# One sink exponential per banded step, one key group on another score bank, final scales two additions sooner

## The reference

```
q,k,v = rope(rmsnorm(x) @ w_in)            # banded heads a, differential heads b
# banded attention: m = max(max_k s, sink)
p     = exp(s - m);  denom = sum(p) + exp(sink - m)
oa    = (p / denom) @ v                    # 8 heads, 2 key/value heads, window of 3 chunks of 64
# differential attention: a = softmax(s1) - lam * softmax(s2);  ob = rmsnorm(a @ v)
h = x + concat[oa, ob] @ w_out
h = h + crossattn(rmsnorm(h), memory)      # 4 heads, 256 memory rows
h = h + square(relu(rmsnorm(h) @ w_up)) @ w_down
y = rmsnorm(h) * g_final
```

## Time and profile before

| what | value |
|---|---|
| median of the runs | 1824.55 us (1822.61 to 1825.99) |
| the profiled execution's own time | 1830.64 us |
| its span | 1828.8 us |
| PE busy | 1745.8 us (95%) |
| DVE busy | 879.7 us (48%) |
| ACT busy | 547.3 us (30%) |
| POOL busy | 179.6 us (10%) |

### The profile page before, as it was taken

One profiled execution on the slowest core, in us unless ns is written; L12 is line 12 of the kernel. 1 busy time (PEld: TensorE's weight loads), 2 busy tenths in 40 slices (PEclk: granted clock), 3 DMA queues, 4 the chain that ended last, 5 costly groups with the idle time before them and its releaser, 6 DMA issues.

```text
span 1828.8 us, 29483 instructions
## 1 busy us (share of the span) xinstructions
PE 1745.8 (95%) x11905; PEld 1612.9 (88%) x11905; DVE 879.7 (48%) x1707; ACT 547.3 (30%) x1216; POOL 179.6 (10%) x355
## 2 busy tenths in 40 slices
PE   6998989997898999989999999999999999999997
PEld 6997989886787999988799999999999999999996
DVE  5556656665466345124323644444444444444445
ACT  5123344576555123025402422111111222112212
POOL 2113322112122001100000000000000000000002
PEclk9999999999999999999999999999999999999999
DMA  6322322254575406256151101111011111110102
GB/s 214 108 67 60 87 85 87 76 164 163 178 235 205 138 24 247 94 187 226 53 197 47 47 27 43 46 46 46 24 45 46 46 46 46 46 46 25 56 1 104
DMA packets 107533, 170.40 MB, mean 93 GB/s; under 512 B 7545, under 2 KB 75769, under 8 KB 107417
## 3 DMA queue, kind: packets, MB, share of 16 engines
q1 hardware_dynamic: 79512, 126.78, 20.4%
q0 software_dynamic: 8160, 22.29, 3.6%
q10 hardware_dynamic: 19760, 19.92, 3.4%
HBM read 138.17 MB, written 31.72 MB: 93 GB/s over the span
## 4 chain that ended last, share of the span: by engine, by line
PE 87%; DVE 4%; ACT 3%; issue 2%; DMA 2%; POOL 1%; SPq 0%; ACTq 0%; DVEq 0%; POOLq 0%
PE banks L2023 27%; PE banks L1977 24%; PE banks L2412 21%; PE banks L2178 2%; PE banks L2121 2%; PE banks L2300 2%; PE banks L2248 1%; PE banks L1965 1%; PE banks L2208 1%; PE banks L2280 1%; PE banks L2269 1%; ACT probs L1285 1%; DMA w_raw<-in_cache_mem_k 1%; PE banks L2158 1%; DVE xt_lo L1478 1%
## 5 line engine op out<-in xcount | busy, mean ns | idle before, releaser
L1977 PE MATMUL banks<-w_hi,xt_hi 128*128 128x256 f32 x1224 | 354.7, 290 | 17.2 <-DVE xt_lo L1478 4.8
L1977 PE MATMUL banks<-w_lo,xt_hi 128*128 128x256 f32 x1224 | 344.7, 282 | 0.0
L1977 PE MATMUL banks<-w_hi,xt_lo 128*128 128x256 f32 x1224 | 344.5, 281 | 0.0
L2023 PE MATMUL banks<-xt_hi,w_hi 128*128 128x384 f32 x960 | 323.0, 336 | 0.0
L2023 PE MATMUL banks<-xt_hi,w_lo 128*128 128x384 f32 x960 | 322.7, 336 | 0.0
L2023 PE MATMUL banks<-xt_lo,w_hi 128*128 128x384 f32 x960 | 322.6, 336 | 0.0
L1977 PEld LDWEIGHTS banks<-w_hi,xt_hi 128*128 128x128 f32 x1224 | 232.6, 190 | 26.2 <-issue 8.9
L1090 ACT ACTIVATE w_hi<-w_raw 128x2048 fp32r<-128x2048 f32 (+1 forms) x85 | 120.2, 1430 | 418.8 <-PE banks L2412 225.8
L1901 DVE TENSOR_TENSOR h<-h,banks 128x512 f32<-128x512 f32 x288 | 191.9, 683 | 98.9 <-PE banks L2412 96.8
L1977 PEld LDWEIGHTS banks<-w_lo,xt_hi 128*128 128x128 f32 x1224 | 232.9, 190 | 0.0
L1977 PEld LDWEIGHTS banks<-w_hi,xt_lo 128*128 128x128 f32 x1224 | 232.7, 190 | 0.0
(11 more groups left out here) (220 smaller groups left out, 2215.4 us busy)
## 6 DMA issues: line engine op xcount, KB each, us to landing
w_raw<-in_w_up SPq DMA_DIRECT2D x16, 1024.0 KB, 5.4
w_raw<-in_w_down SPq DMA_DIRECT2D x16, 1024.0 KB, 4.9
w_raw<-in_w_xkv ACTq DMA_DIRECT2D x8, 1024.0 KB, 6.1
kc_diff<-in_cache_diff_k SPq DMA_DIRECT2D x16, 512.0 KB, 5.6
vc_diff<-in_cache_diff_v SPq DMA_DIRECT2D x8, 1024.0 KB, 5.4
w_raw<-in_cache_mem_k SPq DMA_DIRECT2D x16, 512.0 KB, 7.6
w_raw<-in_w_in ACTq DMA_DIRECT2D x7, 1024.0 KB, 5.3
scaled<-mix_d SPq DMA_DIRECT2D x9, 512.0 KB, 5.2
```

What stands on the lines that cost most here:

```text
L1977: last = mm(out, xt[:, k, tok:tok + P], w[:, k, :], start=(k == 0 and n == 0), stop=(k == KD - 1 and n == 2))
L2023: last = mm(out, w[:, k, :], xt[:, k, tok:tok + CH], start=(k == 0 and n == 0), stop=(k == KD - 1 and n == 2))
```

## The change

The four exponentials of the sinks in a banded step of the prompt become one over four columns. For that DVE adds the sinks to the negative maxima of all four heads (a new tile `sunk`, a new semaphore `s_sunk`), behind the second half's minimum. The streams' banded steps keep theirs. The fourth group of head 2 goes to bank 1, with the waits that this bank needs. The final scales of tiles 3 to 7 stand elsewhere among the last additions.

```diff
@@ banks of the key groups
+PREP[I_D2 - 1][1] = (PREP[I_D2 - 1][1][0], 1)
@@ build
         esink = sb("esink", [P, 4, 4])
+        sunk = sb("sunk", [P, 4, 4])
...
+        s_sunk = sem("s_sunk")
@@ prepared_on
-            on = [n for n, (m, _, b) in enumerate(PREP_LIST) if I_D2 <= m < i < I_X and b in score_banks(i, j)]
-            last = [[n for n in on if (PREP_LIST[n][1][0] == "mem") == low][-1:] for low in (False, True)]
+            on = [n for n, (m, _, b) in enumerate(PREP_LIST) if I_D2 - 1 <= m < i < I_X and b in score_banks(i, j)]
+            last = [[n for n in on if (PREP_LIST[n][1][0] in ("mem", "head")) == low][-1:] for low in (False, True)]
@@ exps (ACT)
-                        if kind in ("swa", "swas"):
-                            at = 4 * j + 2 * y + g
-                            sk = sink[:, at:at + 1] if kind == "swa" else sink_row[:, :]
-                            last = nc.scalar.activation(esink[:, i % 4, c:c + 1], sk, ACT.Exp, bias=bias)
+                        if kind == "swas":
+                            last = nc.scalar.activation(esink[:, i % 4, c:c + 1], sink_row[:, :], ACT.Exp, bias=bias)
+                    if kind == "swa" and j == 1:
+                        act.wait_ge(s_sunk, SWA_NO[i] + 1)
+                        last = nc.scalar.activation(esink[:, i % 4, 0:4], sunk[:, i % 4, 0:4], ACT.Exp)
@@ row_max (DVE)
                         V.tensor_tensor(nm, nm, ns, ALU.min).then_inc(s_negmax, 1)
+                        if kind == "swa" and j == 1:
+                            dve.wait_ge(s_negmax, H_AT[i] + 2)
+                            V.tensor_tensor(sunk[:, i % 4, 0:4].rearrange("p (j g) -> p j g", j=2),
+                                            negmax[:, i % 4, 0:4].rearrange("p (j g) -> p j g", j=2),
+                                            sink[:, :].rearrange("p (j n) -> p j n", j=2)[:, :, 2 * y:2 * y + 2],
+                                            ALU.add).then_inc(s_sunk, 1)
@@ group (DVE)
-                add_down(g * 3 + 1, odd, 1)
-                add_down(g * 3 + 2, odd, 2, {d: (lambda d=d: final_scale(3 + d // 2)) for d in (1, 3, 5)} if last else None)
+                finals = [{4: lambda: final_scale(3)},
+                          {d: (lambda t=t: final_scale(t)) for d, t in ((0, 4), (2, 5), (4, 6), (5, 7))}]
+                add_down(g * 3 + 1, odd, 1, finals[0] if last else None)
+                add_down(g * 3 + 2, odd, 2, finals[1] if last else None)
...
-            for t in range(6, TT):
-                final_scale(t)
+            final_scale(TT - 1)
@@ prep (PE)
-                if b < 4 and PREP_LIST[n][0] in range(I_D2, I_X):
+                if b < 4 and PREP_LIST[n][0] in range(I_D2 - 1, I_X):
                     pe.wait_ge(s_exp, halves_on(b, PREP_LIST[n][0]))
```

More of the change, by code:

```diff
@@ L63 @@
 DIFF_NO = {STEP_NO[s]: n for n, s in enumerate(DIFF)}
+SWA_NO = {STEP_NO[s]: n for n, s in enumerate(SWA)}
 I_LAST = STEP_NO[DIFFS[-1]]
```

## The result

The changed kernel takes 1836.75 us (median of five runs, 1834.96 to 1842.27) where the kernel before, run beside it, took 1825.99 (1822.61 to 1827.82). The ratio is 1.0065, with an interval of 1.005 to 1.0081: it is slower, by some 11 us, where 1821.3 was forecast. The profiled execution took 1842.27, the longest of the five; its span is 1840.5.

What follows compares the result with a forecast made beforehand. PE, busy 95% of the span, was taken as the bound, with gains only where it or the end waits. Sinks 1.27, bank 0.6 and end 1.4 sum to 3.27 us, giving 1821.3, range 1817.8 to 1824.3.

Steps and rivals of the forecast that it cites:

- scores of step 16 to 19: Banded steps 16 and 18: PE waits less for sink exponentials, gaining 0.5 and 0.23 us.
- step 28 to 30: Around steps 28 and 29: two DVE additions of 0.19 less 0.23 idle cost 0.15 us.
- last matmul to the end: Program end: moved scales free POOL's last pair from waiting for DVE, gaining 1.4 us despite an addition 0.45 late.
- What bounds the kernel: Whole kernel: PE busy 95% of the span; changes pay only where PE or the program's end waits for them.
- 1.27 + 0.6 + 1.4: Gains in us from the sinks, the bank in head 2 and the end, 3.27 in all.
- Steps 35, 37 and 38 get 0.23 each: Last banded steps: DVE's sum comes 0.23 us earlier per step, 0.69 in all; step 36 gets nothing.
- The waits that bank 1 adds ... cost nothing: Second stream key group and step 41: added waits are for work done before step 40 begins, costing nothing.
- DVE's delay of 0.19: Last banded steps: the added DVE operation delays what is queued behind by 0.19 us, out of an idle 0.52.
- Rival A: Program end does not gain: POOL's slow operations are its own, only the late addition remains; 1823.1 us, chance 0.17.
- POOL's lock: Program end: DVE with two SBUF inputs and POOL share a port; strewn scales each hold up a POOL pair.
- Rival B: Half-clock places at 390 to 392 and 406.74 us: one or both stay at full clock; about 1819, chance 0.23.
- Rival C: Banded steps: DVE becomes the bound, 0.19 in each of 16 steps costs 3.0; 1825.8 us, chance 0.10.

Runs made afterwards that it cites:

- behind_xt: Kernel before with 64 unused bytes allocated behind xt_hi and xt_lo: 1826.95 against 1826.45 us, ratio 1.0003.
- all_shift64: Kernel before with 64 unused bytes allocated ahead of all tiles: 1826.68 us, ratio 1.0008.
- shift256: Kernel before with 256 unused bytes where the change puts sunk: 1824.78 us, one run.
- shift512: Kernel before with 512 unused bytes where the change puts sunk: 1826.46 us, one run.
- sunk_last: Changed kernel with sunk allocated behind all other tiles: 1823.76 us against 1826.55 of the kernel before, ratio 0.9982.
- shift128: Changed kernel with 64 unused bytes behind sunk, so xt lies 128 bytes higher than before: 1837.02 against 1826.55 us, ratio 1.0055.

## Why the prediction was wrong

By its own steps, on PE's starts from one mark to the next, medians of the kernels with the old code and `xt` in a good place (before, behind_xt, all_shift64, shift256, shift512) and of three with the changed code (after, sunk_last, shift128):

| stretch | old | changed | difference | forecast |
|---|---|---|---|---|
| scores of step 16 to 19 | 19.55 | 18.49 | -1.06 | -0.73 |
| step 28 to 30 | 13.40 | 13.33 | -0.07 | +0.15 |
| step 36 to 38 (the sinks of step 35) | 10.93 | 11.18 | none within its spread | -0.23 |
| step 38 to 39 (the sinks of step 37) | 4.48 | 4.26 | -0.22 | -0.23 |
| step 39 to 40 (the sinks of step 38, the bank) | 6.96 | 6.59 | -0.37 | -0.83 |
| in head 3 | 36.03 | 36.36 | +0.33 | 0 |
| last matmul to the end | 13.70 | 12.24 | -1.46 | -1.4 |

The rows add up to -2.85; the forecast's sum was -3.27, and `sunk_last` measured 2.8 below before. So the sum was nearly right for what it counted, but in part by luck: five of the seven rows miss by 0.22 to 0.46, two to the good and three to the bad, and the time, with an interval from 0.7 to 5.8 us of gain, could not have told 2.85 from 3.27.

**The step that failed** is the first sentence of "What bounds the kernel": *"a change to DVE, ACT and a bank's name can only pay where PE, or the end of the program, waits for them"*. It took PE's own busy time as given, and so the sum, 1.27 + 0.6 + 1.4, has operations, waits and the places of instructions in it and no term for the added tile `sunk`, neither a cost nor a reason for none. The runs showed in its place that PE's own work became longer: 2880 matmuls came every 0.1765 us in place of 0.1734, and 3672 every 0.1182 in place of 0.1171. The tile cost 13 us, four times the whole sum (sunk_last to changed kernel, 1836.75 - 1823.76, in two sets of runs in which before took 1825.99 and 1826.55). No rival could have caught it, since all of them were about the same operations, and the chance of 0.05 for slower had only "a little for what I do not see".

Smaller misses. *"Steps 35, 37 and 38 get 0.23 each"*: the sinks of step 35 did make the stretch from step 36 to 37 shorter, by 0.27 (5.36 to 5.09), but then PE stands before the first key group of head 2 for its load:

```profile
393.83 0.63 PE L2134 MATMUL banks<-ident,head_raw 128*128 128x128 f32 x4 [1.41 <-DMA head_v<-out_diff_v_prompt]
```

The row means what it says: this group's queries and keys share one semaphore with the values of head 2 (`s_head_in`, which PE asks to be at 48, three loads of 16), and the values come last. In the changed kernel the loads of `head_raw` are issued at 384.58 and 385.00, and its four loads land 3.7 to 5.0 us after their issue, so these two by 390.0; the load of the values is on the chain of waits:

```profile
386.96 6.74 DMA head_v<-out_diff_v_prompt
```

It lands at 393.7. PE waits for values that it does not need until later; no run gave them a semaphore of their own. The old code has the same wait wherever PE was at full clock here, 0.90 to 1.28 in the other seven traces of it (median 1.20), and 0.95 to 1.78 in the nine of the changed code (median 1.43): most of what the sinks of step 35 gave is waited out here. In the kernel before that wait was hidden by the half clock of the earlier trace rows, so no row showed that a transfer is next late.

*"The waits that bank 1 adds ... cost nothing"*: they are indeed long satisfied, but they are not only at the two places that the forecast named. Twelve were added, and asking for them behind the exponentials' semaphore costs PE 0.33 in head 3. *DVE's delay of 0.19 "out of an idle 0.52"*: true of step 38, not of step 39, where without the bank's part 0.14 reached PE; so the stretch to step 40 has the bank's 0.5 less 0.14, not 0.83.

Rival A (the end does not gain) is refuted by the rows of the end. What the forecast made of POOL's lock holds. By the Trainium skill's page "SBUF — State Buffer", section "Who interferes with whom", a DVE instruction with two SBUF inputs and a GpSimd instruction that reads SBUF share one port, and the second to start waits for all of the first. The trace agrees: beside the scales now strewn among the additions POOL's first operation takes 0.90 instead of 0.19 and ends at 1823.80, where the scale ends at 1822.47 + 1.28 = 1823.75; this is off the path.

The span's end hangs on POOL's drain, as the forecast had it. In the 17 traces POOL's drain ends 8.35 or 8.36 behind the end of POOL's last operation, though it is 9.52 long with the old end and 8.60 with the new, and the span ends 0.23 to 0.25 behind that. The store behind the last scale is not what counts: SP's drain starts anywhere from 9.56 to 9.79 behind PE's last matmul in the eight kernels with the old end, whose span ends 13.70 or 13.71 behind it.

Rival B (the clock) did not decide it. From 386 to 412 us the granted clock was 1.00 in the changed kernel, but also in `behind_xt`, `all_shift64` and `shift256`, which have the old code, and with `sunk` last it was 0.50 from 396 to 400; so the two half-clock places of the kernel before are not what the change takes away. Stretches at half clock fall at other places from trace to trace (between 389 and 427 us in the kernel before, from 418 to 439 in the changed one), and from step 40 on they hide differences of a microsecond or two. Rival C (DVE as the bound) is seen at one step, 39, with 0.14.

Two slips in the forecast's sums change nothing: 64 exponentials of 0.285 are 18.2, not 18.3, and B's price for one place is 1.7 by its own terms, not 1.6.

## What to carry to other kernels

A new tile is part of a change, however small: it moves every tile behind it, and in this kernel, where PE is busy 95% of the span, 2% on its matmuls (13 us) outweighed all that a few waits gave (3 us). When the same instructions take longer all over a program, compare counts in a window that the diff does not touch, and then try the tile alone and the code alone. Where a wait asks for several semaphores, ask last for the one that comes last: here it made one stretch 0.6 us shorter, too little to be seen in the time.

## What the runs showed of the hardware

The pace of PE's matmuls depends on the distance of their two operands in SBUF, taken by 256 bytes (tried in steps of 32, and 256 and 512 bytes more): with both 4 bytes wide, 384 moving columns came every 173.3 to 176.7 ns and 256 columns every 116.9 to 119.9, at the full granted clock, with places 32 bytes apart alternating in no order that we can give. The Trainium skill's page "SBUF — State Buffer", section "Who interferes with whom", says that PE's two read ports, for the moving operand and for the weights, are independent and that PE waits on no one. A pace that changes by 2 to 2.5% with the distance of the two operands does not come out of that, and the measurement decides. What in the reads meets is open: no run separates the weight load from the moving read. The 512-column products, whose operands keep a distance of a multiple of 256 in all kernels, stayed within 0.2269 and 0.2275.

One more: where PE alone sets the pace, a stretch can be the same to 0.01 us from kernel to kernel. The MLP took 775.41 us in seven kernels with `xt` 224 past, with the old code and the changed one, and 782.77 or 782.78 in the changed kernel and in the one with 64 unused bytes. `behind_xt` is an exception that is not explained: 774.76, with the `down` products 226.9 ns apart in place of 227.4, although both operands of these keep their distance.
